# GpSimd's first loads wait for the fourth modulation block to land, and two groups of them change places

## What is computed

```python
def adaln(cond, w, b):
    m = jax.nn.silu(cond) @ w + b
    return m.reshape(cond.shape[:-1] + (1, 6, D_MODEL))

def modulate(x, g, shift, scale):
    return rmsnorm(x, g) * (1 + scale) + shift

# layer 0
m_lat = adaln(c, w_mod[i], b_mod[i])
h = modulate(x, g_norm1[i], m_lat[..., 0, :], m_lat[..., 1, :])
m_ctx = adaln(c_ctx, w_mod[i], b_mod[i])
hc = modulate(xc, g_norm1[i], m_ctx[..., 0, :], m_ctx[..., 1, :])
y, yc = even_mixer(h, hc, ctx_next, w_in_even[e], w_out_even[e], ...)
x = x + m_lat[..., 2, :] * y
h = modulate(x, g_norm2[i], m_lat[..., 3, :], m_lat[..., 4, :])
x = x + m_lat[..., 5, :] * ec_moe(h, w_router[i], w_exp_gate[i], w_exp_up[i], w_exp_down[i])
```

## Time and profile before

| | us |
|---|---|
| median of 3 runs | 2541.84 |
| the three runs | 2539.03 to 2548.28 |
| the profiled execution's own time | 2544.99 |
| its span, first to last instruction | 2543.2 |
| TensorE busy in the span | 2108.4 (83%) |
| VectorE / ScalarE / GpSimd busy | 914.9 / 744.0 / 104.5 |
| mean granted TensorE clock | 0.923 |

### The profile page before, as it was taken

The page is one execution under the profiler, slowest core; times in us unless marked ns, Lnnn a source line. Parts: engine busy times, 40 slices in busy tenths (PEclk is TensorE's granted clock), DMA queues, the critical chain, the costliest instruction groups (busy, mean ns, idle before and its releaser), DMA issues.

```text
span 2543.2 us, 36110 instructions
## 1 busy us (share of the span) xinstructions
PE 2108.4 (83%) x16306; PEld 1508.8 (59%) x16306; DVE 914.9 (36%) x1314; ACT 744.0 (29%) x1128; POOL 104.5 (4%) x140
## 2 busy tenths in 40 slices
PE   4997976666668776566659999979999999999999
PEld 2764542222223532222219988968998998877997
DVE  4655430000002320000025446666445444445533
ACT  3433310000001200000015446346445444364542
POOL 2100000000000000000000101000100100000110
PEclk8999987888889797888889999989999999999999
DMA  8369779999999399999994544206555555543542
GB/s 281 116 220 387 287 333 425 427 427 428 427 427 414 130 429 427 428 428 427 428 391 159 176 156 159 90 21 207 172 190 184 174 185 200 187 166 127 180 163 102
DMA packets 200025, 679.28 MB, mean 267 GB/s; under 512 B 7952, under 2 KB 101296, under 8 KB 175552
## 3 DMA queue, kind: packets, MB, share of 16 engines
q1 hardware_dynamic: 195328, 664.49, 67.3%
q0 software_dynamic: 2496, 7.24, 0.8%
q10 hardware_dynamic: 2048, 5.24, 0.6%
HBM read 675.90 MB, written 1.05 MB: 266 GB/s over the span
## 4 chain that ended last, share of the span: by engine, by line
PE 57%; DMA 34%; DVE 5%; ACT 3%; SPq 1%; issue 1%; DVEq 0%; ACTq 0%
PE ps L253 45%; DMA ring<-in_w_exp_down 11%; DMA ring<-in_w_exp_gate 11%; DMA ring<-in_w_exp_up 7%; DMA ring<-in_w_mod 4%; PE ps L1858 2%; PE ps L2611 2%; DVE ring_r L679 2%; PE ps L1873 1%; PE ps L782 1%; PE ps L611 1%; PE ps L1919 1%; ACT ring_r L670 1%; DMA ring<-in_ffn_wgu 1%; PE ps L620 1%
## 5 line engine op out<-in xcount | busy, mean ns | idle before, releaser
L253 PE MATMUL ps<-HH,ring_r 128*128 128x256 f32 x2720 | 536.0, 282 | 5.5 <-DVE ring_r L679 3.3
L253 PEld LDWEIGHTS ps<-HH,ring_r 128*128 128x128 f32 x2720 | 434.8, 188 | 9.7 <-DVE ring_r L679 4.2
L1858 PE MATMUL ps<-ring,XS 128*32 128x256 f32 x4096 | 295.8, 440 | 155.4 <-DMA ring<-in_w_exp_gate 111.6
L679 DVE TENSOR_TENSOR ring_r<-ring,ring_r 128x2048 fp32r<-128x2048 f32 (+2 forms) x152 | 325.5, 2180 | 182.9 <-ACT ring_r L670 182.8
L1858 PEld LDWEIGHTS ps<-ring,XS 128*32 128x32 f32 x4096 | 138.6, 123 | 338.3 <-DMA ring<-in_w_exp_gate 164.8
L253 PE MATMUL ps<-HL,ring_r 128*128 128x256 f32 x1136 | 318.6, 280 | 0.0
L670 ACT ACTIVATE ring_r<-ring 128x2048 fp32r<-128x2048 f32 (+2 forms) x152 | 269.2, 1821 | 143.2 <-PE ps L253 90.6
L1873 PE MATMUL ps<-ring,AT 128*32 128x512 f32 x960 | 161.6, 810 | 136.3 <-DMA ring<-in_w_exp_down 133.5
L2082 ACT ACTIVATE SG<-ps 128x256 f32<-128x256 f32 x32 | 12.3, 383 | 819.6 <-PE ps L1858 808.6
L253 PEld LDWEIGHTS ps<-HL,ring_r 128*128 128x128 f32 x1136 | 214.0, 188 | 0.3 <-issue 0.2
L1973 DVE TENSOR_TENSOR AA<-SG,ps 128x256 f32<-128x256 f32 x32 | 13.5, 422 | 518.8 <-PE ps L1858 518.8
(11 more groups left out here) (556 smaller groups left out, 2876.0 us busy)
## 6 DMA issues: line engine op xcount, KB each, us to landing
ring<-in_w_exp_gate SPq DMA_DIRECT2D x64, 2048.0 KB, 35.8
ring<-in_w_exp_up SPq DMA_DIRECT2D x64, 2048.0 KB, 36.2
ring<-in_w_exp_down SPq DMA_DIRECT2D x64, 2048.0 KB, 36.5
ring<-in_ffn_wgu SPq DMA_DIRECT2D x88, 1024.0 KB, 7.7
ring<-in_w_mod SPq DMA_DIRECT2D x24, 2048.0 KB, 13.9
ring<-in_ffn_wd SPq DMA_DIRECT2D x20, 2048.0 KB, 7.8
ring<-in_odd_w_in SPq DMA_DIRECT2D x12, 2048.0 KB, 8.0
ring<-in_even_w_in SPq DMA_DIRECT2D x6, 2048.0 KB, 8.0
```

The costliest lines, as they stand in the source:

```text
L253: ins = e.matmul(out, l, r, start=start and i == 0, stop=stop and i == n - 1, skip_group_check=True)
L679: v.tensor_tensor(lo[:, c], s[:, c], hi[:, c].bitcast(F32), ALU.subtract).then_inc(*E.up("split_dve", name, q))
L1858: ins = e.matmul(self.GU[which][32 * j:32 * j + 32, :], self.XS[:, 4 * hk + k, 32 * n:32 * n + 32], W[:, k, 256 * j:256 * j + 256], start= ...
```

## The change

GpSimd waits for the landing of modulation block 3 (the semaphore of slot 5 at 16) ahead of its first DMA. The 8 loads of `pool_loads` are now issued before the 18 of `start.pool`. Every other instruction, on every engine, is as before.

```diff
     def gpsimd(self, g):
         S, E, w = self.S, self.S.E, Waits(g)
+        w.wait_ge(E.at("loaded", ("mod", 0, 3)))
+        self.even.pool_loads(g)
         self.start.pool(g, w)
-        self.even.pool_loads(g)
         self.even.pool(g, w)
```

## The result

The changed kernel takes 2535.74 us (median of 19 runs, 2532.19 to 2540.44), the kernel before 2541.24 (19 runs beside them, 2539.03 to 2551.91). The ratio is 0.9977 (95% interval 0.9971 to 0.9983): 5.8 us less by the ratio, between 4.3 and 7.4 (5.5 by the two medians). The profiled execution took 2537.93 us with a span of 2536.1. That is within 0.5% and inside the range, as forecast, but more than the 3.8 us of the sum.

The account below looks back on a forecast made before the run. The prediction took the DMA transfers of `w_mod` up to block 3's landing as the bound. With all other effects costed at nothing, 2541.84 - 3.8 = 2538.0 us, range 2532 to 2546.

Parts of the forecast that it names:

- What bounds: Start of the kernel: the chain lies on `w_mod` transfers until block 3 lands at 38.10 us, with DMA engines 99.4% full.
- The size of the first term: Block 3's landing: moving GpSimd's loads behind it frees 4.04 us of engine time, worth 3.8 us; landing at 34.3 us.
- The upper bound: Before block 3: 3.7 us by bytes plus 1.3 us if small loads cause the 317 GB/s from 8 to 16 us: 5.0.
- The reading by share: Up to block 3's landing: software queue's 10.6% of 38.1 us is 4.04 us, divided by 1.07 gives 3.8 us.
- the small loads drag the others: Rival, 8 to 16 us: small loads slow the other queues, so the gain is 5.0 us, time 2536.8; 10%.
- The estimate from the page on DMA: GpSimd's loads at the start: 18 small ones at 0.68 us plus tables at 3.7 us would win some 16 us.
- What the loads meet: Beside pieces 1280 and 768 of `w_in_even`: at least 2.3 and 2.1 us of cover, so the loads cost nothing there.
- a lost cover: At pieces 1280 and 768: without cover, each microsecond of lateness would come straight off the gain.
- Who waits for the loads: Later readers and GpSimd's `QK` scaling: all covered, tables by over 40 us, so the later issues cost nothing.
- the two rivals about GpSimd's issues and VectorE: GpSimd's issues hold up VectorE, adding 15.0 us, 2553.0, 3%; or VectorE holds back issues, tables late at L1112, 2555.8, 2%.
- The clock: Rival, TensorE's clock falls elsewhere: gates' product at half level, gain 1.4 us, 10%; or faster block 3 products, 4.9 us, 8%.
- The issue of the blocks as the limit: Rival at block 3: SyncE's issue, up to 10.96 us, sets the landing; it stays at 38.1, time 2541.8; 9%.

Follow-up runs that it names:

- the wait alone: Changed kernel with GpSimd's wait kept but its loads in the old order, 18 small ones first, tables behind: 2536.1 us, ratio 0.9981 to the kernel before.
- the wait for 768: Changed kernel with GpSimd waiting for piece 768 of `w_in_even` in place of block 3: 2535.72 us, ratio 0.9974 to the kernel before.
- one group late at a time: Two edits of the changed kernel: only the 18 small loads wait for block 3, 2540.91 us; only the 8 table loads wait, 2538.48 us.
- The kernel with SyncE waiting: Changed kernel with SyncE too waiting for block 3 before issuing the first pieces of `w_in_even`: 2538.41 us, ratio 0.9992 to the kernel before.
- the doubled load: Kernel before with two more GpSimd loads, 1.43 MB, behind the old ones, run in two series: 2548.22 us (ratio 1.0023) and 2544.71 us (1.0011).

## Why the prediction came out as it did

**What bounds.** Right. The transfers up to block 3 set the start, and what is taken out of them comes off the end nearly one to one: block 3 lands at 38.5 us on average in two profiles of before and at 32.7 in four that wait in full (the change twice, the wait alone, the wait for 768), 5.8 us earlier, and the end moved by 5.8 (4.3 to 7.4).

**The size of the first term.** This step failed: 3.8 us, where 5.8 was measured, and 3.8 lies outside the interval. The upper bound of 5.0 is short of 5.8 too, but inside the interval. That the time came out within 0.5% and inside the range of 2532 to 2546 says nothing for the term: a gain of nothing would have done the same. The reading by share fails on its premise that a queue costs what its own packets take. The software queue's 4.04 us count no part of the time by which it lengthened the packets of the others. The upper bound had the right mechanism, "the small loads drag the others", to which I gave 10%, but two wrong inputs. It took 377 GB/s as the full rate, from a stretch that holds the 64-byte packets of piece 2816 (305 GB/s from 36 to 38 us), where the changed kernel shows 396 from 8 to 16 us. And it began at 8 us, while the rate from 2 to 8 us is 336 GB/s before and 358 after. With these, 1.40 MB at 387 GB/s is 3.6 us, the stretch from 8 to 16 us gives (396 - 317) x 8 / 396 = 1.6, the one before it (358 - 336) x 6 / 358 = 0.4: 5.6 us.

The total fits the 5.8 us; its parts are less sure. With one group late at a time, the landings give the tables 38.48 - 33.94 = 4.5 us, 0.9 more than their bytes, and the small loads 38.48 - 37.34 = 1.1, less than the 2.0 that the rate gives them. Each of these is one profile, and the tables alone brought the stretch from 8 to 16 us to 330 GB/s. So how the 2 us beyond the bytes divide between the two groups stays open. The prediction's argument against the drag, that the token loads share that stretch, falls: they share it in the changed kernel too, at 396.

**The estimate from the page on DMA.** The Trainium skill's 0.68 us for a 4 KB load (page "DMA: Bandwidth & Descriptors", section "Bandwidth"), as summed there, is far off in the other direction: 32 strided loads of 0.5 KB moved the landing by 35.28 - 32.7 = 2.6 us, 0.08 us each. They overlap: one is issued every 0.54 us and lands 5.6 us after its issue, so a time for one load can't be added up.

**What the loads meet.** Right. Piece 1280 had no idle time ahead of its split, and the wait for 768 shows no cost of the loads there. The kernel with SyncE waiting shows the other side: pieces later by a few microseconds did take the gain back, as the text had it for a lost cover.

**Who waits for the loads.** Right, with its times: the scaling of `QK` at 62.66 (62.9 forecast), L1112 at 93.7 (93.9), the first DMA with the landing. The issue of `sel`, clear of L372 now, takes 0.54 us in place of 0.90. That agrees with the rule of the Trainium skill's page "SBUF — State Buffer", in the box on DVE and DMA; it never came near to a late table. Nothing in the profile speaks for the two rivals about GpSimd's issues and VectorE. Only the expert stage came otherwise: at 352.81 us, where 356 was forecast. The block landed earlier than forecast, and the clock's swing at 281 and 311 us fell on the side of the change in that profile.

**The clock.** Block 3's products met the lower level (3.68 us), in the second profile of the change the full one (1.96). It shifted the profiles by a microsecond or two, as the rival's size said, and the medians by nothing that could be separated. What I had not listed is that the same happens at 281 and 311 us and is worth 4.0 us in one profile.

**The issue of the blocks as the limit.** Excluded: the landing moved by -5.8 and +3.7 us with the load alone, and the long issue ahead of block 3 shrank with it, from 10.96 to 8.00 us.

Open: whether the end moves by somewhat more than the landing (the two series of the doubled load leave 3.0 to 7.4 us for a landing of 3.6 to 4.6), why one program lands its block between 32.0 and 33.4 us, and how the cost beyond the bytes divides between tables and small loads.

## What to carry to other kernels

Loads that are read late belong behind the transfers that the first chain waits for, and the cover is easily had from the trace: the first reader's time less the new landing. For the size of the gain, compare what the other queues move per time beside such loads and without them, in stretches free of other small packets; a queue's own share hides what it does to its neighbours. A difference of a few microseconds between two profiles should be looked for in the granted clock of each stretch before it is given a cause in the code, and a second profile of both kernels shows whether it stays.

## What the runs showed of the hardware that was not expected

- Loads that read single 4-byte numbers a row apart pulled all DMA queues together down from 396 to 313 to 318 GB/s while they were under way, with 16 KB of their own; the same number of loads with 8 adjacent numbers per row, and the same 1024 packets by the profile's count, left 384.
- With the tables (0.97 MB in that stretch) and no small load, the rate from 8 to 16 us was 330 GB/s, also below 396.
- One program landed its fourth 2 MB block at 32.0 or 33.4 us, with the same bytes moved by 33 us (9.63 and 9.64 MB on the weight queue in two of the profiles).
- With nothing queued behind the block, no packet moved from 31.5 to 32.5 us around a landing at 31.72, and the two stretches of 2 us around it read 200 and 77 GB/s: a queue that waits for a landing left the engines idle for over 1 us.
